# Gathering each expert's tokens feature-major instead of token-major

## The reference, cut to what matters

```
def moe_ffn(h, w_router, b_router, w_gate_up, b_gate_up, w_down, b_down):
    logits = h @ w_router + b_router
    top_val, top_idx = lax.top_k(logits, 4)
    weights = softmax(top_val)
    ...                     # tokens are sorted into blocks, each block has one expert e
    xb = h[tok]                                  # gather the block's tokens
    gu = xb @ w_gate_up[e] + b_gate_up[e]
    gate, up = minimum(gu[:, :1024], 7), clip(gu[:, 1024:], -7, 7)
    act = (up + 1) * gate * sigmoid(1.702 * gate)
    y = act @ w_down[e] + b_down[e]
    ...                     # sum of y * weight over the four experts of each token
```

## Time and profile before

| what | value |
|---|---|
| median of the runs | 1793.51 us |
| the profiled execution's own time | 1790.86 us |
| its span | 1789.1 us |
| TensorE matmul busy | 1610.8 us (90%) |
| TensorE weight load busy | 853.6 us (48%) |
| VectorE busy | 381.4 us (21%) |
| ScalarE busy | 297.9 us (17%) |
| DMA, mean over the span | 281 GB/s |

### The profile page before, as it was taken

How to read it: one execution, slowest core, us unless ns; L and a number is a source line. 1 busy time by engine, 2 the same in 40 slices (tenths; PEclk the granted TensorE clock), 3 DMA queues, 4 the chain that set the end, 5 groups by cost and what they waited for, 6 DMA issues and landing times.

```text
span 1789.1 us, 19200 instructions
## 1 busy us (share of the span) xinstructions
PE 1610.8 (90%) x7790; PEld 853.6 (48%) x7791; DVE 381.4 (21%) x692; ACT 297.9 (17%) x470; POOL 49.2 (3%) x89
## 2 busy tenths in 40 slices
PE   6997677876789999999999999999999999999998
PEld 3875466654633333333333333333333387598643
DVE  2335422123231211211111121212121123311002
ACT  2224201111111211211111111111111123100000
POOL 3000111010000000000000000000000000000000
PEclk9999667777779999999999999999999999999999
DMA  9515012203539999999999999999999953343330
GB/s 356 182 47 211 30 65 95 95 0 136 246 156 428 427 429 429 429 428 428 428 428 428 429 428 428 429 429 429 428 428 429 412 212 136 135 148 141 141 141 24
DMA packets 75033, 503.15 MB, mean 281 GB/s; under 512 B 5278, under 2 KB 8496, under 8 KB 50416
## 3 DMA queue, kind: packets, MB, share of 16 engines
q1 hardware_dynamic: 72240, 498.22, 67.9%
q10 hardware_dynamic: 2752, 4.34, 0.7%
HBM read 501.49 MB, written 1.05 MB: 281 GB/s over the span
## 4 chain that ended last, share of the span: by engine, by line
PE 54%; DMA 21%; DVE 2%; ACT 1%; issue 0%; ACTq 0%; SPq 0%; DVEq 0%
DMA ring<-in_w_gate_up 21%; PE psum L922 14%; PE psum L958 8%; PE psum L1168 5%; PE psum L1183 5%; PE psum L990 3%; PE psum L886 2%; PE psum L870 2%; PE psum L513 2%; PE psum L820 2%; PE psum L1125 2%; PE psum L1193 2%; PE psum L915 1%; PE psum L1140 1%; PE psum L1100 1%; PE psum L1006 0%
## 5 line engine op out<-in xcount | busy, mean ns | idle before, releaser
L922 PE MATMUL psum<-ring,work 128*64 128x512 f32 x2048 | 457.5, 597 | 44.2 <-DMA ring<-in_w_gate_up 44.2
L922 PEld LDWEIGHTS psum<-ring,work 128*64 128x64 f32 x2048 | 140.5, 137 | 359.3 <-issue 269.5
L958 PE MATMUL psum<-ring,work 128*64 128x512 f32 x1024 | 226.8, 595 | 1.6
L1871 DVE TENSOR_SCALAR work<-psum 128x512 f32<-128x512 f32 x32 | 22.1, 691 | 628.5 <-PE psum L922 628.5
L958 PEld LDWEIGHTS psum<-ring,work 128*64 128x64 f32 x1024 | 71.2, 137 | 136.7 <-issue 130.2
L1168 PE MATMUL psum<-xT,ring 128*128 128x256 f32 x448 | 96.9, 379 | 0.0
L1429 ACT ACTIVATE work<-work 128x512 f32<-128x512 f32 x32 | 20.1, 630 | 440.6 <-DVE work L1871 440.6
L1168 PEld LDWEIGHTS psum<-xT,ring 128*128 128x128 f32 x448 | 85.0, 190 | 11.5
L576 PE MATMUL psum<-hT,ring 128*128 128x256 f32 (+1 forms) x368 | 80.4, 380 | 2.8 <-ACT hT L1258 2.8
L1183 PE MATMUL psum<-ring 128*128 128x512 f32 x192 | 82.6, 592 | 0.0
L576 PEld LDWEIGHTS psum<-hT,ring 128*128 128x128 f32 (+1 forms) x368 | 68.3, 186 | 15.0 <-ACT hT L1258 3.1
(11 more groups left out here) (392 smaller groups left out, 1472.2 us busy)
## 6 DMA issues: line engine op xcount, KB each, us to landing
ring<-in_w_gate_up SPq DMA_DIRECT2D x128, 2048.0 KB, 32.0
ring<-in_w_down SPq DMA_DIRECT2D x72, 2048.0 KB, 35.3
ring<-in_w_ada SPq DMA_DIRECT2D x12, 2048.0 KB, 10.5
ring<-in_w_up SPq DMA_DIRECT2D x8, 2048.0 KB, 7.5
ring<-in_w_in SPq DMA_DIRECT2D x6, 2048.0 KB, 11.1
ring<-in_w_out SPq DMA_DIRECT2D x4, 2048.0 KB, 7.7
ring<-in_w_in_sb SPq DMA_DIRECT2D x4, 2048.0 KB, 22.6
ring<-in_w_mem_kv SPq DMA_DIRECT2D x1, 2048.0 KB, 9.1
```

The costliest lines, as they stand in the source:

```text
L922: ins = mm(B(1 + u)[CAP * h:CAP * (h + 1), :], xe[:, k % 4, k // 4, :], w[:, k % 2, c0:c0 + 512], start=False, stop=k == KT - 1)
L958: last = mm(B(3)[CAP * h:CAP * (h + 1), :], act[:, k % 4, k // 4, :], w[:, k % 4, 512 * h:512 * (h + 1)], start=k == 0, stop=k == KT - 1)
```

## The change

TensorE's gather is turned round. The token matrix becomes the stationary operand, with every fourth feature taken (128 columns, a step of 4 elements, which is 16 bytes), and the selection mask of 64 slots is the moving operand. The result is feature-major at once: for each `c` and `h` a block of 128 features by 64 slots, laid out in the bank as `xe` has it. The transposes `turn_x` are gone, and so are the reordering copy `x_out` with the buffer `x_tm`. The one copy that stays, `xe_out`, now waits for the gather. The data loads and their order, VectorE's work, and all other products are the same. Nothing is computed otherwise than before but for the layout.

```
-                for ti in range(TT):
+                for c in range(4):
                     for h in range(2):
-                        last = mm(B(0)[CAP * h:CAP * (h + 1), :], sel[:, ti, :],
-                                  tok[:, ti, 512 * h:512 * (h + 1)], start=ti == 0, stop=ti == TT - 1)
+                        for ti in range(TT):
+                            last = mm(B(0)[:, (2 * c + h) * CAP:(2 * c + h + 1) * CAP],
+                                      tok[:, ti, 512 * h + c:512 * (h + 1):4], sel[:, ti, :],
+                                      start=ti == 0, stop=ti == TT - 1)
                 last.then_inc(S("e_gather"), 1)
-
-            def turn_x(g):
-
-                pe.wait_ge(S("e_xtm"), g)
-                for c in range(4):
-                    last = tr(B(0)[:, c * P:(c + 1) * P], x_tm[:, c * P:(c + 1) * P])
-                last.then_inc(S("e_xturn"), 1)
...
             gather(1)
-            turn_x(1)
...
                         last.then_inc(S("e_selturn"), 1)
-                        turn_x(g + 2)
...
-            def x_out(g):
+            def xe_out(g):
                 ac.wait_ge(S("e_gather"), g)
-                A(by_four(x_tm), B(0).rearrange("p (q c) -> p q c", c=4), ACT.Copy).then_inc(S("e_xtm"), 1)
-
-            def xe_out(g):
-                ac.wait_ge(S("e_xturn"), g)
                 A(xe.rearrange("p c h s -> p (c h s)"), B(0), ACT.Copy).then_inc(S("e_xe"), 1)
...
-            x_out(1)
             xe_out(1)
...
-                x_out(g + 2)
```

More of the change, by code:

```diff
@@ L243, in build @@
         ended = yT[0:1, 2:8, :].rearrange("p a b -> p (a b)").rearrange("p (g e) -> p g e", g=N_ITEM)
-        x_tm = yT[:, 0:2, :].rearrange("p a b -> p (a b)")
         ye = view(work_f, 3584, [512])
```

## The result

The changed kernel takes 1976.85 us (median of 4 runs, 1972.64 to 1978.94) against 1792.85 us for the kernel before: a ratio of 1.1021, 95% interval 1.0999 to 1.1044. It is slower by 184 us. The forecast was 1904 us with a range up to 1960 us, so the direction and the price of the step held roughly, and the granted clock and the size did not.

The account below looks back on a forecast made before the run. Transfers of `w_gate_up` bounded the kernel before; at 213 ns a gather instruction TensorE would, with 32 items of 32.01 us and +1.6 us at the start: 1793.51 + 110 = 1904 us, range 1793 to 1960 us.

Parts of the forecast that it names:

- the price of the step: Gather's weight loads: columns 16 bytes apart advance at 1.67 ns each instead of 0.83, 213 ns an instruction.
- the granted clock: TensorE in the expert items: expected to stay at its full clock throughout.
- What bounds the kernel: Experts: `w_gate_up` transfers set the end before, 29.39 us an item; after the change TensorE, with no load waited for.
- what goes: Removed transposes and reordering copy: 0.0 us saved within an item (0.1 at most), 1.8 us once before the first.
- The sum: Whole kernel at 213 ns an instruction: gather 6.82 us, item 32.01 us, +110 us, 1904 us; chance 0.42.
- the sign: Gather's weight loads at L870: mean near 297 ns if the forecast is right, near 190 if stepping is free.
- The rule on lines of 16 bytes: SBUF reads: full bandwidth needs two hits a line, so a step of 4 float32 pays; 4 fp32 also called free.
- The falling clock: Each item: some 3.4 us, half a gate and up's worth, at half clock; 54 us more, 1958 us; within a 0.15 case.
- more than twice: Gather loads: each column read twice, 427 ns, 2123 us; or the lower clock returns, 1958 us; chance 0.15.
- the forecast's own range: Whole kernel: 1890 to 1920 us, for 205 to 228 ns a gather instruction.
- The start: First gather to first bias product: +3.4 us for the longer gather, less 1.8 saved, +1.6 us.
- The first rival: Gather: step free, 110 ns an instruction, item 28.74 us hidden under transfers, +3.7 us, 1797 us; chance 0.30.

Follow-up runs that it names:

- the three stepped reads: 16-byte steps on the gather's stationary operand (changed kernel, 1976.85 us), its moving operand (kernel before, 1799.04 us) and the token transposes (kernel before, 1791.64 us).
- The filled gather: Changed kernel, 16-byte step kept, but each gather product (save the last block) moves the mask twice, 128 columns: 1932.22 us, ratio 1.0773.
- the packed kernel: Changed kernel with the gather's stationary columns neighbouring instead of 16 bytes apart, features in another order: 1808.75 us, ratio 1.0087.
- the packed runs: Changed kernel with neighbouring stationary columns, once with features left in another order (1808.75 us), once with tokens stored reordered ahead of the experts (1807.22 us).
- the layout put right once: Changed kernel with the copies that fill `tok` reordering features ahead of the experts, so the gather reads neighbouring columns: 1807.22 us, ratio 1.0080.

## Why the prediction was wrong in size

**What bounds the kernel, and what goes: right.** The chain of the changed kernel has no load in it, the transposes' going saved nothing, the down projection still waits for ScalarE's copy of the activation.

**The price of the step: right in kind, a tenth too low, and for a reason that was partly luck.** The sum took 213 ns, 6.82 us; measured 239 ns, 7.66 us. That is 0.84 x 32 = 27 us of the 73 between forecast and measurement. The mean load at L870, named as the sign, is 329 ns and not 297. I had carried over a price of 1.67 ns from ScalarE's and VectorE's stepped writes. If the estimate from the three stepped reads holds, a single read costs about 0.9 ns a column and the product pays twice. Then two errors nearly cancelled: the price of one read was lower, and the number of reads higher. The rule on lines of 16 bytes that I weighed from the Trainium skill (SBUF — State Buffer, section "Door 1: The DMA port swizzle"), at least two hits on a line for full bandwidth, agrees with these runs: two hits on each line cost 122 ns, one costs 239. The same note's phrase that 4 fp32 are free does not.

**The clock: the step that failed.** "The granted clock at full through the items" was wrong, and the sum of an item had no term for it. The falling clock stood among the rivals, in the case "more than twice", as half clock for 3.4 us of gate and up; it came, at 0.50, and its place was the gather's second half and the scatter, where it costs 3.19 - 1.93 = 1.26 us an item, 40 us in all. The filled gather shows that this part is the clock's alone. I had L833 in hand, a long run of loads with few moving columns (32) at a clock of 0.50, and set against it that waits for transfers had never brought the clock down. Those waits were 1.3 us at most (44.2 us in 44), between products that move 512 columns; the gather is 7.7 us of slow loads with 64 columns each.

**The range: too narrow at the top, by 17 us.** It held each effect by itself, and the two come together: 1904 + 27 + 40 = 1971. The 5.6 us ahead of the experts in the profiled run fill most of the rest. Code that no change touches differs by as much between kernels: the first b_down product starts at 499.33 before, at 504.90 after and at 506.19 in the packed kernel. The price in the rival was also badly worked out: half a gate and up is 6.94 us, not 3.4. And 205 ns an instruction gives 1896 us, not the 1890 of the forecast's own range.

**The start: +2.1 against +1.6 us**, since stepped loads take 239 ns at half clock as well (the sum itself gives 7.14 - 3.64 - 1.8 = +1.7).

**The first rival was wrong too**, which the packed runs showed: 1809 and 1807 in place of 1797 us. Its item, 28.74 us in the prediction and 28.91 in the run, was compared with the 29.39 us of a late item in place of the average of 28.66.

## What to carry to other kernels

Count the pieces of 16 bytes that an operand's columns touch. Here a stepped float32 operand of TensorE, stationary or moving, paid for each piece, and a product paid more than a transpose did. Before, the reordering in ScalarE's copy cost nothing on the path, and with the layout put right once the gather's products ran at the packed pace: such places are the cheaper ones. When a load gets slower while the product stays small, ask also for the clock, and price what stands behind it at the half clock, together with the slower load and not as another case. And where transfers start with a lead, compare an engine's item with the average item over the loop, lead included, not with the rate of the transfers: what stays under that is nearly free.

## What the runs showed of the hardware that I had not expected

One recorded instruction of a float32 product with 128 stationary columns: 116 ns packed, 122, 182, 239 and 244 ns at steps of 8, 12, 16 and 32 bytes. At half clock the step of 16 bytes costs the same 239 ns (first gather, 7.66 us), where packed loads go from 116 to 219 ns (7.02 us): the pace of the packed load follows TensorE's clock, that of the stepped one does not. That the memory sets it is an argument, not a record. A transpose's load goes only from 140 to 206 ns. TensorE can count as busy at every moment (3.00 us of 3.00 in the windows above) and still lose its full clock.
